# First modulation sums in quarters, and tile 6 between blocks at the mixer's entry

## What is computed

```python
mods = (silu(c) @ w_ada + b_ada).reshape(9, 1024)      # shift, scale, gate for three sublayers

def sublayer(h, j, fn, resid_w):
    u = layer_norm(h) * (1 + scale_j) + shift_j
    z = ALPHA * h + resid_w * gate_j * fn(u)
    return layer_norm(z) * ln_g[j] + ln_b[j]

h = sublayer(h, 0, swiglu(ffn1), 0.5)      # (silu(u @ w_gate) * (u @ w_up)) @ w_down, width 2816
h = sublayer(h, 1, mixer, 1.0)             # u @ w_in, two kinds of attention, @ w_out
h = sublayer(h, 2, swiglu(ffn2), 0.5)
```

## Time and profile before

| | us |
|---|---|
| median of 3 runs | 1976.26 |
| lowest, highest | 1975.4, 1978.62 |
| profiled execution | 1979.03 |
| its span | 1977.2 |
| TensorE busy | 1902.4 |
| VectorE busy | 1228.4 |
| ScalarE busy | 834.0 |
| GpSimd busy | 605.5 |

### The profile page before, as it was taken

One profiled execution on the slowest core, in us unless ns is written; L12 is line 12 of the kernel. 1 busy time (PEld: TensorE's weight loads), 2 busy tenths in 40 slices (PEclk: granted clock), 3 DMA queues, 4 the chain that ended last, 5 costly groups with the idle time before them and its releaser, 6 DMA issues. The chain is left out here.

```text
span 1977.2 us, 26739 instructions
## 1 busy us (share of the span) xinstructions
PE 1902.4 (96%) x9698; PEld 1528.0 (77%) x9698; DVE 1228.4 (62%) x1987; ACT 834.0 (42%) x1459; POOL 605.5 (31%) x432
## 2 busy tenths in 40 slices
PE   6999999999999989999999998989999999999997
PEld 4778888887888766777678876778888888888886
DVE  5876766665697863444535556688444444457888
ACT  4533333333445663443435554265333333334543
POOL 0253443343960010000043230003534434449500
PEclk9999999999999999999999998999999999999999
DMA  9256565556874421110043113532333332368733
GB/s 332 68 197 195 178 211 162 182 184 215 303 260 119 139 94 44 54 33 32 12 115 69 43 43 107 192 107 62 120 107 95 118 107 86 118 223 295 247 107 117
DMA packets 164667, 271.42 MB, mean 137 GB/s; under 512 B 13012, under 2 KB 83768, under 8 KB 164408
## 3 DMA queue, kind: packets, MB, share of 16 engines
q1 hardware_dynamic: 153888, 235.18, 36.0%
q10 hardware_dynamic: 9624, 30.39, 4.9%
q0 software_dynamic: 1024, 4.13, 1.2%
HBM read 211.73 MB, written 57.93 MB: 136 GB/s over the span
## 5 line engine op out<-in xcount | busy, mean ns | idle before, releaser
L1720 PE MATMUL f_ps<-f_uh,f_ops 128*128 128x512 f32 x2496 | 775.5, 391 | 8.3 <-DVE f_ul L1531 1.9
L1720 PEld LDWEIGHTS f_ps<-f_uh,f_ops 128*128 128x128 f32 x2496 | 469.4, 188 | 112.0 <-issue 10.1
L1720 PE MATMUL f_ps<-f_ul,f_ops 128*128 128x512 f32 x1248 | 486.4, 390 | 0.0
L1082 POOL TENSOR_TENSOR f_sums<-f_raw 128x512 f32<-128x512 f32 x80 | 112.1, 1402 | 529.8 <-DMA f_raw<-in_ffn_w_gate 232.3
L1720 PEld LDWEIGHTS f_ps<-f_ul,f_ops 128*128 128x128 f32 x1248 | 234.6, 188 | 48.3
L1579 DVE TENSOR_TENSOR f_dl<-f_blocks,f_dh 128x1024 fp32r<-128x1024 f32 (+1 forms) x146 | 207.5, 1438 | 69.4 <-ACT f_dh L1289 69.3
L1289 ACT CAST f_dh<-f_blocks 128x1024 fp32r<-128x1024 f32 (+1 forms) x146 | 144.3, 990 | 215.9 <-PE f_ps L1850 213.0
L1403 DVE TENSOR_TENSOR f_ops<-f_sums,f_ops 128x512 fp32r<-128x512 f32 x160 | 125.5, 784 | 119.8 <-ACT f_ops L1143 119.5
L1850 PE MATMUL f_ps<-f_dh 128*128 128x512 f32 x496 | 193.1, 389 | 0.8 <-DVE f_ev L1616 0.8
L1850 PE MATMUL f_ps<-f_dl,f_dh 128*128 128x512 f32 x496 | 193.0, 389 | 0.0
L1850 PE MATMUL f_ps<-f_dh,f_dl 128*128 128x512 f32 x496 | 193.0, 389 | 0.0
(11 more groups left out here) (284 smaller groups left out, 3073.5 us busy)
## 6 DMA issues: line engine op xcount, KB each, us to landing
f_hidden<-acc SPq DMA_DIRECT2D x154, 256.0 KB, 4.3
f_blocks<-f_hidden SPq DMA_DIRECT2D x154, 256.0 KB, 3.3
f_blocks<-in_ffn_w_down SPq DMA_DIRECT2D x132, 256.0 KB, 5.4
f_raw<-in_ffn_w_gate SPq DMA_DIRECT2D x20, 1024.0 KB, 6.2
f_raw<-in_ffn_w_up SPq DMA_DIRECT2D x20, 1024.0 KB, 5.5
f_aw<-in_w_ada ACTq DMA_DIRECT2D x28, 512.0 KB, 4.1
acc<-in_w_ada ACTq DMA_DIRECT2D x28, 512.0 KB, 3.9
in_raw<-in_w_in SPq DMA_DIRECT2D x24, 512.0 KB, 4.0
```

Of the source, the lines that this page charges most:

```text
L1082: nc.gpsimd.tensor_tensor(sums[:, x], of, with_, how).then_inc(s_done, 1)
L1720: done = nc.tensor.matmul(ps[:, bank, :], l[:, k, :], r[:, k, :], start=fresh and k == 0 and m == 0, stop=closed and k == HK - 1 and m == ...
```

## The change

The modulation sums go in four quarters of 256 features (two strips of a bank) instead of two halves; a quarter's weights come in two parts of 512 rows, so each DMA has rows of 256 floats instead of 512. With a quarter the first two feature blocks of half 0 can be modulated. Products 0 to 7 are cut into slices: `plain_slice(kk, k)` multiplies one feature block with four weight blocks, in four banks at once, 12 matmuls; TensorE's order alternates slices, sums, row transposes and transposes. Transposes of half 0 use three banks in turn, those of half 1 four in another order, all eight of them now ahead of product 8; product 8 to 11 wait only for the modulation that frees their own bank. ScalarE's and VectorE's orders follow the quarters. Tiles 4 and 5 of x are loaded ahead of quarter 3, tiles 6 and 7 behind it. The bias table is stored from GpSimd's queue, once quarter 3 has landed.

In the mixer's entry ScalarE makes the deviation of tile 7 between its casts, VectorE the coefficients and the affine of tile 6 inside `blocks(0)`, so that tiles 4 to 6 are normalised together and tile 7 alone; the third product's weights are split on VectorE instead of GpSimd. The square root of tiles 4 and 5 moves from the end of the first phase to the entry.

```diff
+    def load_w(self, sp, q):
+        for c in range(2):
+            if q >= 2:
+                sp.wait_ge(self.summed, 2 * (q - 2) + c + 1)
+            view = self.w_ada[:, HK * c:HK * c + HK, 0:M_FIRST].rearrange("p k (s n) -> p k s n", s=2)
+            for s in range(2):
+                sp.dma_start(self.mem.first_w[2 * (q % 2) + c][:, :, s, :], view[:, :, s, 2 * P * q:2 * P * q + 2 * P]
+                             ).then_inc(self.w_ld[2 * q + c], 16)
+
+    def store_table(self, pool):
+        pool.wait_ge(self.neg, 1)
+        pool.wait_ge(self.w_ld[2 * QUARTERS - 1], 32)
...
+    def bank_of(self, q):
+        return 0 if q == 0 else 5
+
+    def add_products(self, pe, ps, q, c):
+
+        bank = self.bank_of(q)
+        if c == 0:
+            if q < 2:
+                pe.wait_ge(self.zeroed, 1 if q == 0 else 3)
+                pe.wait_ge(self.c_ready, 1)
+            else:
+                pe.wait_ge(self.columns, q)
+        pe.wait_ge(self.w_ld[2 * q + c], 32)
+        for k in range(HK * c, HK * c + HK):
+            for j in range(2):
                 done = self.nc.tensor.matmul(ps[32 * j:32 * j + 1, bank, 0:2 * P], self.cs[:, k:k + 1],
...
-        @block.gpsimd
-        def _(pool):
-            pool.wait_ge(w_hi, 3)
-            nc.gpsimd.tensor_tensor(wl[:, :, 0, :], raw[:, :, 0, :], wh[:, :, 0, :].bitcast(F32),
-                                    ALU.subtract).then_inc(q_lo, 1)
...
+            def entering(t, first):
                 act.wait_ge(closing.shifted, t + 1)
                 ent.mean(act, t, t + 1, t - 2)
                 ent.square(act, t, acc[:, t, :])
-            ent.root(act, 6, 8)
-            for t in (6, 7):
-                ent.normalise(act, t, acc[:, t, :], 3)
+                ent.root(act, first, t + 1)
+
+            split(2)
+            for y in range(5):
+                high(y)
+            closing.deviation(act, 7, ent.nrm[7])
+            for y in range(5, KT):
+                high(y)
+            split(1)
+            entering(6, 4)
+            split(0)
+            for t in (4, 5, 6):
+                ent.normalise(act, t, acc[:, t, :], 2)
+            entering(7, 7)
+            ent.normalise(act, 7, acc[:, 7, :], 3)
...
+                    if y == 5:
+                        closing.coefficients(dve, 6)
+                        closing.affine(dve, 6)
...
             split(1, 2)
-            ent.coefficients(dve, 4, 6, 2)
-            for t in (6, 7):
-                closing.coefficients(dve, t)
-                closing.affine(dve, t)
-            ent.coefficients(dve, 6, 8, 3)
+            ent.coefficients(dve, 4, 7, 2)
+            split(0, 3)
+            closing.coefficients(dve, 7)
+            closing.affine(dve, 7)
+            ent.coefficients(dve, 7, 8, 3)
...
-        TURN = (6, 7, 2, 5)
+        TURN = (6, 7, 2, 5), (2, 5, 6, 7)
...
+        def turn_bank(y):
+            if begin is not None and y < KT:
+                return TURN[0][y % 3]
+            return TURN[y // KT][y % 4]
...
+                begin.load_w(sp, 0)
             load_part(0)
             if begin is not None:
-                for i in range(3):
-                    begin.load_w(sp, 1, i)
+                begin.load_w(sp, 1)
+                begin.load_w(sp, 2)
             load_part(1)
...
-                begin.load_w(sp, 1, 3)
-                begin.load_x(sp, TT // 2, TT)
-                begin.store_table(sp)
+                begin.load_x(sp, TT // 2, 6)
+                begin.load_w(sp, 3)
+                begin.load_x(sp, 6, TT)
...
+                begin.store_table(pool)
+                pool.wait_ge(begin.ln.normed, TT)
+                pool.wait_ge(begin.columns, QUARTERS)
...
+                    y = max(x for x in range(KT, 2 * KT) if turn_bank(x) == PLAIN_BANK[half][j][f])
+                    pe.wait_ge(mod_done[y % 2], y // 2 + 1)
...
+            def plain_slice(kk, k, these=range(4)):
+
+                pe.wait_ge(lo0, HK * kk + k + 1)
+                u = (B11, B21)[kk]
+                for n in these:
+                    o = 4 * kk + n
+                    pe.wait_ge(w_lo, o + 1)
...
+                turn(0)
                 begin.turn_rows(pe, ps, 0)
+                turn(1)
+                turn(2)
+                plain_slice(0, 0)
+                begin.add_products(pe, ps, 1, 0)
+                begin.add_products(pe, ps, 1, 1)
+                plain_slice(0, 1, (0, 1))
+                begin.turn_rows(pe, ps, 1)
+                turn(3)
+                plain_slice(0, 1, (2, 3))
+                begin.add_products(pe, ps, 2, 0)
+                plain_slice(0, 2, (0, 1))
+                begin.add_products(pe, ps, 2, 1)
+                plain_slice(0, 2, (2, 3))
+                begin.turn_rows(pe, ps, 2)
+                turn(4)
+                turn(5)
+                plain_slice(0, 3)
+                plain_slice(1, 0)
+                begin.add_products(pe, ps, 3, 0)
+                begin.add_products(pe, ps, 3, 1)
+                plain_slice(1, 1, (0, 1))
+                begin.turn_rows(pe, ps, 3)
+                turn(6)
+                turn(7)
+                plain_slice(1, 1, (2, 3))
+                plain_slice(1, 2)
+                plain_slice(1, 3)
+                for y in range(KT, 2 * KT):
                     turn(y)
+                for p in range(RING, PLAIN):
+                    plain_product(p)
```

More of the change, by code:

```diff
@@ L243, in normalise @@
                                   scale=self.part(self.R, t, t + 1)).then_inc(self.normed, 1)
+QUARTERS = 4
 class Beginning:
@@ L349, in turn_rows, with take @@
-    def turn_rows(self, pe, ps, h):
-        pe.wait_ge(self.taken, h + 1)
+    def take(self, dve, ps, q):
+        dve.wait_ge(self.summed, 2 * q + 2)
+        if q >= 1:
+            dve.wait_ge(self.turned, q)
+        self.nc.vector.tensor_copy(self.rows[:, :], ps[:, self.bank_of(q), 0:2 * P]).then_inc(self.taken, 1)
+    def turn_rows(self, pe, ps, q):
+        pe.wait_ge(self.taken, q + 1)
         for b in range(2):
-            done = self.nc.tensor.transpose(ps[:, (0, 5)[h], 2 * P + P * b:2 * P + P * b + P],
+            done = self.nc.tensor.transpose(ps[:, self.bank_of(q), 2 * P + P * b:2 * P + P * b + P],
@@ L1378, in _ @@
                 ent.square(act, 5, acc[:, 5, :])
-            if ent is not None:
-                ent.root(act, 4, 6)
-            else:
+            if ent is None:
                 closing.deviation(act, 7)
@@ L1705, in turn @@
                 pe.wait_ge(normed, TT // 2 * (y // KT + 1))
-                if y >= 4:
-                    pe.wait_ge(mod_done[y % 2], (y - 4) // 2 + 1)
+                if begin is not None and y == KT:
+                    pe.wait_ge(begin.columns, QUARTERS)
+                if turned_before(y) is not None:
+                    pe.wait_ge(mod_done[turned_before(y) % 2], turned_before(y) // 2 + 1)
                 k = y if y < KT else half1(y)
                 for g in range(TT // 2):
-                    done = nc.tensor.transpose(ps[:, TURN[y % 4], P * g:P * g + P],
+                    done = nc.tensor.transpose(ps[:, turn_bank(y), P * g:P * g + P],
                                                nrm[y // KT][:, g, P * k:P * k + P], ident[:, :])
@@ L1740, in plain_product @@
                 multiply(PLAIN_BANK[half][j][f], o, uh[:, high], ul[:, low], kk == 0, kk == 1, split, had)
+            def plain_slice(kk, k, these=range(4)):
[4 more added lines that the diff above has]
+                    pe.wait_ge(w_lo, o + 1)
+                    _, _, j, f = plain(o)
+                    wh, wl = op(o)
+                    for m, (l, r) in enumerate(((wh, uh), (wh, ul), (wl, uh))):
+                        done = nc.tensor.matmul(ps[:, PLAIN_BANK[0][j][f], :], l[:, k, :], r[:, u, k, :],
+                                                start=kk == 0 and k == 0 and m == 0,
+                                                stop=kk == 1 and k == HK - 1 and m == 2, skip_group_check=True)
+                    if k == HK - 1:
+                        done.then_inc(mm, 1)
             def product(j, i):
```

156 lines of the change are left out of this document (64 added, 92 removed).

## The result

| | median of the runs | lowest to highest | profiled execution | its span |
|---|---|---|---|---|
| before | 1975.79 us (12 runs) | 1972.28 to 1978.62 | 1979.03 | 1977.2 |
| after | 1980.43 us (12 runs) | 1978.92 to 1984.58 | 1978.92 | 1977.1 |

What follows compares the result with a forecast made beforehand. VectorE's chain, not TensorE, was taken to bound the first 120 us. +2.4 us (beginning) and -3.5 us (mixer's entry) sum to -1.1, from a median of 1976.26 to 1975.2 us; range 1971.0 to 1980.0.

Steps and rivals of the forecast that it cites:

- What bounds it now: First 120 us: VectorE's chain, not TensorE, is late last; earlier TensorE products only lengthen its wait at 101.31 us.
- Part 1: Loads up to 44 us: 1 KB rows run at 349 instead of 387 GB/s, 2.3 us more; quarter 3 at 43.6.
- Rival C: Loads: 1 KB rows cost nothing, quarter 3 lands at 41.3; total 1972.9 us; chance 0.07.
- Part 2: TensorE before token 4: products begin about 4 us earlier, sums stay 64, no matmul added; costed at nothing.
- Part 3: Tokens 4 to 7: from quarter 3 at 43.6, transposes start at 56.4 and ScalarE's first modulation at 57.6.
- Part 4: Bias table issued on POOL from 43.7 lands at 59.4, gating ScalarE's modulation, late by 1.8 us against 57.6.
- Rival E: Bias table: VectorE holds up POOL's issues, 19.5 instead of 8.4 us; sum +5.0, total 1981.3 us; chance 0.12.
- Part 5: Tokens 4 to 7: fourth low part ends at 67.4, 2.4 us late; first part +2.4, bounds 0 to +4.5.
- Part 6: Mixer's entry: transposes at 715.1 instead of 718.01 without waiting, 0.5 more from full clock; -3.5 us, bounds -1 to -4.
- rival F: Mixer's entry: tile 6 between blocks costs what it gives, -0.5 instead of -3.5; total 1978.2 us; chance 0.08.
- Sum: Whole kernel: +2.4 for the first part and -3.5 for the mixer's entry give -1.1 us, median 1975.2.

Runs made afterwards that it cites:

- with four strips: Changed kernel with each quarter's sums spread over four 32-column strips instead of two, even and odd input blocks in strips of their own: 1976.78 us, ratio to before 1.0004.
- the beginning by its own runs: Changed kernel with the mixer's entry put back as before, so only the beginning's change remains: 1984.68 us, ratio to before 1.0043, +8.5 us.
- the new entry alone: Kernel before with only the change's part in the mixer's entry: 1975.65 us, ratio to before 0.9998.
- with the table later: Changed kernel with sums over four strips and the bias table's sixteen transfers issued by SP behind x tiles 6 and 7: 1977.73 us, ratio to before 1.0010.

## Why the prediction was wrong

**What bounds it now.** Right for before: only an earlier start of VectorE's chain counts, and the 7.06 us at the chain's head came through to the mixer's entry undiminished. But the same thought was used to cost TensorE at nothing, and that is the step that failed.

**Part 1, the loads.** The mechanism was right, the size a little too small. Quarter 3 was taken by the forecast at 43.6; GpSimd saw it land at 44.5, and at 44.1 with four strips. Rows of 1 KB alone made the last sums 2.64 us late where the term had 2.3. At the product wait it was 3.42, with half clock in it that the term did not have. Rival C is false here: 349 against 387 GB/s for the smaller row. By the Trainium skill (DMA: Bandwidth & Descriptors, Specifications) 512 bytes suffice for line rate; the measurement decides against it.

**Part 2, TensorE.** "The split into blocks adds no matmul; sums stay 64", costed at nothing, and 0.5 us in part 3 for the last of them. The count was right and the price doubled, because a quarter's shift and scale fill only two strips. 96 sums that would take 5.9 us took 11.0, so that TensorE, not the landing of quarter 3, set when its sums ended: 51.49 instead of 44.1. The 1.04 us for 16 in the earlier trace rows was a rate of products that overlap; the term should have asked what the overlap hangs on. This is the main error: with four strips the product wait came 3.42 us earlier, of the 4.66 us (7.06 less 2.4) by which the beginning was missed. Some of the 3.42 is the clock's (0.7 us at the transposes): in five of the six profiles with the new beginning TensorE was at half clock for some us between 23 and 28, behind a wait of 2.0 to 2.4 us (in the sixth it stayed full behind 2.00), and no term had that either.

**Part 3, when tokens 4 to 7 are ready.** With four strips the chain can be laid beside the forecast step by step: last sums from 43.75 (43.6), statistics of tile 7 at 52.41 (50.9), transposes at 57.84 (56.4). From the sums on it is 1.4 to 1.5 us late, and the sums explain it: 1.91 us for all 32 in one group instead of 0.5 for the last part, since TensorE reached them only at 43.75, with the second part about to land. In the changed kernel the row stood at 63.69.

**Part 4, the table.** Masked in the changed kernel, whose transposes came late enough; with four strips it gated, at 61.47 instead of 59.4, and by 2.4 us instead of 1.8. Issue time right (8.39 us); from first issue to landing 17.4 us instead of 15.7. The slip is in the sum itself: 0.75 MB at 48 GB/s are 15.6 us, not "some 14"; with 15.6 it gives 61.6. Rival E, issues held up by VectorE, did not come: 8.38 us for the sixteen, with VectorE busy 1.97 of the 2 us from 45 to 47 (subtractions and statistics). No run here puts other kinds of VectorE instruction beside the issues.

**Part 5.** With four strips the fourth low part ended at 68.60 (forecast 67.4) and the product waited at 104.95 (103.7): from the low part to the product it is 36.4 us where the forecast had 36.3, from ScalarE's first modulation to the low part 7.1 instead of 8.0. In the changed kernel the two stand at 72.01 and 108.37.

**Part 6, the entry.** TensorE not waiting ahead of the transposes: right. The low parts 1.1 us late: they stopped TensorE for 2.03 to 2.73 us. The slack that I counted, 2.08 us of VectorE's ahead of block 6's modulation, was that of one profile: in the five others with the old entry it is 0.16 to 0.83 us. And the reference was the second slowest of six entries, 41.77 against a mean of 40.69, with TensorE's clock at half from 691 to 697 us. Worth 1.2 us instead of 3.5; rival F (-0.5, a chance of 0.08) named this mechanism and was the nearest for the entry.

**Sum.** +7.06 - 1.2 = +5.9 by the traces; +8.5 - 1.2 = +7.3 with the beginning by its own runs (8.5, interval [5.9, 11.1]); measured +4.6 [3.2, 6.1]. From the first product of attention to the end the thirteen profiles take 1241.2 to 1248.0 us, so two single spans (1977.2 and 1977.1) can hide 5 us. That this is all chance isn't shown: the six profiles with the new beginning average 1242.4 there, the seven with the old one 1244.9, and 2.5 us given back would bring the traces' sum to +3.4. The attentions are the same code in both; only the second feed-forward phase has other banks and another order of transposes. What it is stays open.

Rival E's total, +5.0, is the nearest to the measured +4.6, by luck: what it is made of, a table 6 us later, did not happen. The range's upper end, 1980.0, was short because the bound of the beginning, +4.5, held no term for TensorE at all.

No kernel here beats before beyond its interval: the new entry alone is the nearest, 0.9998 [0.9988, 1.0007].

## What to carry to other kernels

A price taken from overlapping instructions holds only for the same overlap: before costing "the same number of matmuls", ask how many strips of the array they spread over. When an edit takes away a wait of the engine that is not bound, work out what that engine now has to do before the next hand-over, since it may become the bound. And an entry or stage that varies by 2 us from one execution to another can't be costed against one of them.

## What the runs showed of the hardware that I had not expected

- One-column products of 256 columns follow each other every 0.054 us over four 32-column strips (1.04 us for 16, 1.91 for 32) and every 0.108 us over two (1.89, 3.62), at full clock; three orders of visiting four strips gave 1.04, 1.06 and 1.07 us.
- Transfers out of 8 partitions (48 GB/s alone) slow others: with them among the weights the engines moved 182 to 287 GB/s at a busy share of 0.88, and in before 226 and 227 at 0.99 to 1.00 from 43 to 47 us.
- SP's sixteen issues of the table took 5.43 us from 32.63 in before and 15.44 us from 38.65 with the table later; GpSimd's 8.38 to 8.39 in four kernels.
- VectorE's subtractions of two SBUF operands took 1.76 and 1.77 us beside GpSimd's additions and 0.68 behind them, GpSimd's additions 1.61 to 1.72 instead of 1.27. The Trainium skill (SBUF — State Buffer, SBUF: two separate sides) has a lock on a shared port pair for this; these rows agree with it in direction.
